# A conditioned decoder layer step on one core: masks and first weights loaded in prompt attention, window keys loaded by position class

## What is computed

```
h = RMSNorm(x) * (1 + scale1) + shift1          scale, shift, gate = silu(c) @ w_ada, split in 6
qa,ka,va,qb,kb,vb,logf,ga,gb = split(h @ w_in)  qa, ka rotated; ga, gb through a sigmoid
A: 3 groups x 4 heads, window and dilation (128,1), (512,4), (2048,16); combined by denominators
   sample rows: query t reads kv[lw + t - d*j], j = 0..window/d, from cache_a1, cache_a2, cache_a3
B: 8 heads, causal, bias = sum of logf between key and query
   sample rows: 16 pages of 128 keys per sequence, picked by page_table from cache_b_k, cache_b_v
mix = (ga * (oA @ w_pa) + gb * (oB @ w_pb)) @ w_o
x   = x + gate1 * RMSNorm(mix);  then a hierarchical mixture of 32 experts, 2 per row
```

## Time and profile before

| what | value |
|---|---|
| median of 3 runs | 1197.81 us (1197.62 to 1199.43) |
| profiled execution, its own time | 1199.27 us |
| its span | 1197.5 us |
| PE busy | 1000.1 us, 84% of the span |
| DVE, ACT, POOL busy | 379.9, 206.0, 187.3 us |
| mean granted clock of PE | 0.91 of full speed |
| read from HBM, written | 335.46 MB, 63.36 MB |

### The profile page before, as it was taken

One profiled execution on the slowest core, in us unless ns is written; L12 is line 12 of the kernel. 1 busy time (PEld: TensorE's weight loads), 2 busy tenths in 40 slices (PEclk: granted clock), 3 DMA queues, 4 the chain that ended last, 5 costly groups with the idle time before them and its releaser, 6 DMA issues. The chain is left out here.

```text
span 1197.5 us, 17987 instructions
## 1 busy us (share of the span) xinstructions
PE 1000.1 (84%) x7324; PEld 585.3 (49%) x7324; DVE 379.9 (32%) x865; ACT 206.0 (17%) x509; POOL 187.3 (16%) x210
## 2 busy tenths in 40 slices
PE   3999999997897169979989997579977998777770
PEld 2444444444564046647656674136554554444430
DVE  3100033237751164516701771003451222100105
ACT  3000000014542011100020003001231211111114
POOL 0000033311200100022222311100003322212110
PEclk9999999999997589989989998669978999989995
DMA  9976666977787779998969984979187999999966
GB/s 339 355 278 248 249 248 248 326 244 255 256 212 168 207 240 213 289 349 322 370 231 334 364 320 151 391 266 341 57 325 269 364 370 383 379 393 394 397 256 237
DMA packets 98062, 348.48 MB, mean 291 GB/s; under 512 B 13018, under 2 KB 56802, under 8 KB 78654
## 3 DMA queue, kind: packets, MB, share of 16 engines
q1 hardware_dynamic: 80478, 265.90, 64.8%
q0 software_dynamic: 15552, 79.97, 18.1%
q10 hardware_dynamic: 1952, 1.48, 0.5%
HBM read 335.46 MB, written 63.36 MB: 333 GB/s over the span
## 5 line engine op out<-in xcount | busy, mean ns | idle before, releaser
L1605 PE MATMUL bank<-turned,w_all 128*128 128x320 f32 (+1 forms) x512 | 143.7, 425 | 0.0
L442 PE MATMUL bank<-w_all,turned 128*128 128x481 f32 (+2 forms) x384 | 119.3, 503 | 1.1 <-DVE turned L651 1.1
L442 PE MATMUL bank<-w_ring,turned 128*128 128x481 f32 (+2 forms) x384 | 118.4, 502 | 0.0
L2013 PE MATMUL bank<-w_all,mix_row 128*64 128x256 f32 x736 | 92.2, 407 | 26.9 <-DMA w_all<-in_w_exp 25.8
L1605 PEld LDWEIGHTS bank<-turned,w_all 128*128 128x128 f32 x512 | 95.3, 196 | 35.6 <-issue 15.5
L2013 PEld LDWEIGHTS bank<-w_all,mix_row 128*64 128x64 f32 x736 | 60.9, 147 | 65.3 <-issue 46.4
L1709 DVE STREAM_TRANSPOSE mods<-w_all 128x2048 f32<-128x2048 f32 (+1 forms) x39 | 86.6, 2239 | 9.8 <-PE bank L1481 7.1
L442 PEld LDWEIGHTS bank<-w_all,turned 128*128 128x128 f32 (+1 forms) x384 | 56.8, 171 | 61.5 <-issue 58.3
L442 PEld LDWEIGHTS bank<-w_ring,turned 128*128 128x128 f32 (+1 forms) x384 | 57.1, 171 | 60.4 <-issue 57.3
L2059 DVE COPY act_t<-bank 128x128 f32<-128x128 f32 x33 | 9.6, 292 | 200.8 <-PE bank L2023 199.1
L661 DVE COPY w_all<-bank 128x481 f32 (+5 forms) x32 | 16.9, 531 | 152.6 <-PE bank L442 152.4
(11 more groups left out here) (357 smaller groups left out, 1318.5 us busy)
## 6 DMA issues: line engine op xcount, KB each, us to landing
w_all<-in_w_exp SPq DMA_DIRECT2D x22, 2048.0 KB, 41.0
out_a_sample<-in_cache_a SPq DMA_DIRECT2D x8, 4080.0 KB, 21.4
w_all<-in_w_exp SPq DMA_DIRECT2D x25, 1024.0 KB, 39.2
mods<-in_w_ada SPq DMA_DIRECT2D x21, 1024.0 KB, 8.8
w_all<-in_cache_a SPq DMA_DIRECT2D x96, 128.0 KB, 7.5
w_all<-in_cache_a SPq DMA_DIRECT2D x40, 256.0 KB, 6.1
turned<-in_w_exp SPq DMA_DIRECT2D x5, 2048.0 KB, 42.2
mods<-in_w_exp SPq DMA_DIRECT2D x5, 2048.0 KB, 43.7
```

The costliest lines, as they stand in the source:

```text
L442: mm = nc.tensor.matmul(m.banks[i][r:r + ROWS[i], 0:hi - lo], m.hT[:, k, i * P:i * P + ROWS[i]], ring[u][:, CW * k + lo:CW * k + hi], star ...
L1605: mm = nc.tensor.matmul(GATE[:, 0:WIDTH[h]], gate_w[b][k][:, c % 2 * P:(c % 2 + 1) * P], m.hT[:, k, 256 * h:256 * h + WIDTH[h]], start=k = ...
L2013: mm = nc.tensor.matmul(m.banks[2 + p][x * SLOTS:(x + 1) * SLOTS, 0:HID], hgT[:, k, :], m.weights(u)[:, (2 * k + x) * HID:(2 * k + x + 1) ...
```

## The change

1. `window_keys_in` takes one residue and one position class of all four sequences per DMA: destination 128 partitions of 256 columns, source [4 sequences, 32 positions, 256]. The number of DMAs stays at 8 per window (4 for the half one), as do their 128 KB.
2. Masks, the gate weights of pair 0 and its merge weights are issued by SP in phase_b, between and behind the early key windows, after a wait for the last turn of the prompt's tiles. The mask input holds the four copies, so it is one DMA. The weights lie in slices of 6 per row tile and not of 7.
3. DVE computes the page row numbers in the first value step, and waits for masks and constants only where a mask is added.
4. The gate pieces start at step 1.

```diff
@@ -113,6 +113,7 @@
+        m.wmask = m.low[4][:, 0:13 * P]
...
@@ -127,6 +128,8 @@
+        m.gate_in = [ctx.enter_context(nc.semaphore(f"gate_w{b}")) for b in range(2)]
+        m.merge_in, m.mask_in = [ctx.enter_context(nc.semaphore(n)) for n in ("merge_w", "mask_rows")]
         with ExitStack() as attn:
...
@@ -212,7 +215,7 @@
-            "mask_window": np.concatenate(window, axis=1), "sample_consts": sample_consts,
+            "mask_window": np.tile(np.concatenate(window, axis=1), (4, 1)), "sample_consts": sample_consts,
...
@@ -245,11 +248,26 @@
 def window_keys_in(eng, I, slot, arrived, u, g):
     name, t, t0 = window_of(g)
     n = min(t, 2)
-    for j in range(4):
-        src = I[name][4 * u + j].rearrange("(c i t) n -> i t c n", c=4, t=t)[:, t0:t0 + n, :, 0:AH * HD]
-        dst = slot[32 * j:32 * j + 32, 0:n * 4 * AH * HD].rearrange("p (t c n) -> p t c n", t=n, c=4)
-        for x in range(n):
-            eng.dma_start(dst[:, x], src[:, x]).then_inc(arrived, 16)
+    src = I[name][4 * u:4 * u + 4].rearrange("s (c i t) n -> s i t c n", c=4, t=t)[:, :, t0:t0 + n, :, 0:AH * HD]
+    for x in range(n):
+        for c in range(4):
+            dst = slot[:, (4 * x + c) * AH * HD:(4 * x + c + 1) * AH * HD]
+            eng.dma_start(dst, src[:, :, x, c]).then_inc(arrived, 16)
+
+
+def gate_weights_in(eng, I, m, p, b):
+    src = I["w_gates"][2 * b + p // 2].rearrange("p (k n) -> p k n", k=KD)[:, :, (p % 2) * 256:(p % 2 + 1) * 256]
+    for lo, hi in ((0, 6), (6, 8)) if b == 0 else ((0, 4), (4, 8)):
+        at = (8 * b + lo) % 6
+        dst = m.low[(8 * b + lo) // 6][:, at * 256:(at + hi - lo) * 256]
+        eng.dma_start(dst.rearrange("p (k n) -> p k n", n=256), src[:, lo:hi, :]).then_inc(m.gate_in[b], 16)
+
+
+def merge_weights_in(eng, I, m, p):
+    cols = slice(256 * p, 256 * (p + 1))
+    for name, lo, hi in (("w_pa", 16, 18), ("w_pb", 18, 22)):
+        dst = m.low[lo // 6][:, lo % 6 * 256:(lo % 6 + hi - lo) * 256].rearrange("p (k n) -> p k n", n=256)
+        eng.dma_start(dst, I[name].rearrange("p (k n) -> p k n", n=D)[:, :, cols]).then_inc(m.merge_in, 16)
 
...
@@ -857,6 +875,14 @@
             for k in range(1, KV_RING - 1):
                 early_keys(k)
                 piece(BEFORE + 1 + k)
+                if k == 2:
+                    sp.dma_start(m.wmask, I["mask_window"]).then_inc(m.mask_in, 16)
+                    sp.wait_ge(turn_a, len(turns))
+                    sp.wait_ge(turn_d, len(turns))
+                    gate_weights_in(sp, I, m, 0, 0)
+                if k == 3:
+                    gate_weights_in(sp, I, m, 0, 1)
+            merge_weights_in(sp, I, m, 0)
 
         @block.gpsimd
         def _(pool):
...
@@ -1230,7 +1256,7 @@
             pieces += [("gate", c, h, 0, 0), ("gate", c, h, 0, 4)]
         for c, h in parts:
             pieces += [("gate", c, h, 1, 0), ("gate", c, h, 1, 4), ("out", c, h, 0, 0)]
-    FIRST, END = 3, 80
+    FIRST, END = 1, 80
...
@@ -1262,16 +1288,16 @@
         share = sb("shares", [P, 4])
-        wmask = m.low[4][:, 0:AT * P]
+        wmask = m.wmask
...
         sc_b = m.sc.rearrange("p (h n) -> p h n", h=2)
-        slices = [m.low[i][:, 256 * x:256 * (x + 1)] for i in range(4) for x in range(7)]
+        slices = [m.low[i][:, 256 * x:256 * (x + 1)] for i in range(4) for x in range(6)]
         gate_w = [slices[0:8], slices[8:16]]
         wp_a, wp_b = slices[16:18], slices[18:22]
-        th_a = {x: slices[22 + x] for x in range(4)}
-        th_b = slices[26:28]
+        th_a = {x: m.low[x][:, 1536:1792] for x in range(4)}
+        th_b = slices[22:24]
         flat_wa = m.wa[:].rearrange("p u f q -> p (u f q)")
         mix = [kept[:, 0], kept[:, 1], *(flat_wa[:, 512 * x:512 * (x + 1)] for x in range(3)), *(m.low[4][:, 512 * x:512 * (x + 1)] for x in range(3))]
...
@@ -1294,7 +1320,7 @@
-        gate_in, wp_in = [sem(f"gate_w{b}") for b in range(2)], sem("merge_w")
+        gate_in, wp_in = m.gate_in, m.merge_in
...
@@ -1337,22 +1363,12 @@
                 (window_keys_in if part == "k" else window_values_in)(sp, I, m.ring[slot_of[n]], arrived(n), own(u), g)
 
             def gate_weights(p, b):
...
+                sp.wait_ge(gate_pe, sum_of[(2 * p - 1, 1, b)] + 1)
+                gate_weights_in(sp, I, m, p, b)
 
             def merge_weights(p):
...
+                sp.wait_ge(out_pe, 4 * p)
+                merge_weights_in(sp, I, m, p)
 
             def past_bias(u, x):
                 if (own(u), x) == (0, 0):
...
@@ -1368,12 +1384,7 @@
 
             sp.dma_start(pt_col[:], I["page_table"].rearrange("a n -> n a")).then_inc(pcol_in, 16)
             window(KV_RING - 1)
-            gate_weights(0, 0)
-            for j in range(4):
-                sp.dma_start(wmask[32 * j:32 * j + 32, :], I["mask_window"]).then_inc(con_in, 16)
             sp.dma_start(consts[:], I["sample_consts"]).then_inc(con_in, 16)
-            gate_weights(0, 1)
-            merge_weights(0)
             sp.dma_start(page_ids, I["page_table"].rearrange("a n -> (a n)").partition_broadcast(P)).then_inc(pages_in, 16)
             sp.dma_start(run_id[:], I["run_ids"]).then_inc(pages_in, 16)
             for t in range(N):
...
@@ -1588,7 +1599,7 @@
-                    pe.wait_ge(wp_in, 48 * (c // 2 + 1))
+                    pe.wait_ge(wp_in, 32 * (c // 2 + 1))
                     pe.wait_ge(gated, 2 * i)
...
@@ -1720,6 +1731,9 @@
+                    dve.wait_ge(m.mask_in, 16)
+                    if c == 3:
+                        dve.wait_ge(con_in, 16)
                     cols = slice(512 * c, 512 * c + (512 if c < 3 else P))
                     ins = add(sc_a[:, cols], S(u, c)[:, 0:cols.stop - cols.start], wmask[:, cols], peak[:, 0, c:c + 1])
                     if c == 3:
...
@@ -1824,14 +1838,15 @@
+            def rows_of_pages():
+                dve.wait_ge(pages_in, 16 * 2)
+                for j in range(4):
+                    rows = slice(32 * j, 32 * j + 32)
+                    for dst, ids in ((key_rows, page_ids[rows].rearrange("p (u s g) -> p u s g", u=2, s=4)[:, :, j, :]),
+                                     (value_rows, page_ids[rows].rearrange("p (s x g) -> p s x g", s=NSEQ, x=4)[:, :, :, j])):
+                        V.tensor_scalar(dst[rows].rearrange("p (a b) -> p a b", a=ids.shape[1]), ids, 32.0, run_id[rows, 0:1], ALU.mult, ALU.add).then_inc(idx_ok, 1)
+
             turn(0)
-            dve.wait_ge(pages_in, 16 * 2)
-            for j in range(4):
...
-            dve.wait_ge(con_in, 16 * 5)
             for t in range(N + 1):
                 for x in piece_at.get(t, []):
                     if x[0] == "out":
...
@@ -1846,6 +1861,8 @@
                         if kind(u) == "b":
                             add_bias(u, 4)
                         maxima(u)
+                    if (u, part, g) == (0, "v", 0):
+                        rows_of_pages()
                     if (u, part, g) == (0, "v", 1):
                         running_sums()
                     if part == "v" and g == 3:
```

More of the change, by code:

```diff
@@ L1339, in gate_weights @@
             def gate_weights(p, b):
[L1340 to L1345, removed]
-            def merge_weights(p):
[L1348 to L1355, removed]
+                sp.wait_ge(gate_pe, sum_of[(2 * p - 1, 1, b)] + 1)
+                gate_weights_in(sp, I, m, p, b)
+            def merge_weights(p):
+                sp.wait_ge(out_pe, 4 * p)
+                merge_weights_in(sp, I, m, p)
             def past_bias(u, x):
@@ L1826, in _ @@
             use_dve = {"shares": shares, "fold": out_cols, "totals": past_sums}
-            turn(0)
-            dve.wait_ge(pages_in, 16 * 2)
-            for j in range(4):
-                rows = slice(32 * j, 32 * j + 32)
-                for dst, ids in ((key_rows, page_ids[rows].rearrange("p (u s g) -> p u s g", u=2, s=4)[:, :, j, :]),
-                                 (value_rows, page_ids[rows].rearrange("p (s x g) -> p s x g", s=NSEQ, x=4)[:, :, :, j])):
-                    V.tensor_scalar(dst[rows].rearrange("p (a b) -> p a b", a=ids.shape[1]), ids, 32.0, run_id[rows, 0:1], ALU.mult, ALU.add).then_inc(idx_ok, 1)
-            dve.wait_ge(con_in, 16 * 5)
+            def rows_of_pages():
[5 more added lines that the diff above has]
+                        V.tensor_scalar(dst[rows].rearrange("p (a b) -> p a b", a=ids.shape[1]), ids, 32.0, run_id[rows, 0:1], ALU.mult, ALU.add).then_inc(idx_ok, 1)
+            turn(0)
             for t in range(N + 1):
```

## The result

The changed kernel takes **1256.38 us** (median of 4 runs, 1253.85 to 1258.95) against 1198.62 us before (4 runs, 1197.62 to 1203.24): a ratio of 1.0474, 95% interval 1.0435 to 1.0513. It is slower, as forecast, and by nearly the forecast amount (1259 us). The profiled execution took 1258.95 us, its span 1257.1.

The account below looks back on a forecast made before the run. The prediction took PE, busy 84% of the span, to bound the kernel, with its longest idle stretch outside the expert part 27.70 us. It summed 1199.3 + 61, less 1.5 for the median, to 1259 us, range 1225 to 1340.

Parts of the forecast that it names:

- Four engines: Key loads: each new key DMA runs on 4 DMA engines, the same four each time, 32 pieces each.
- The price of a window: Key loads: a key window on four engines takes 13 us, between 11.8 and 19.6, against 4.9 before.
- for four engines that walk like rows in step: Key loads: a little added to the 11.8 us window in taking 13 us.
- Step 1: Prompt attention: slice 15 of `w_ada` there at 418, next phase begins at 427 and not 395.0, +32 us.
- The moved loads: Prompt attention: masks and gate weights, 2.95 MB ahead of the last slices of `w_ada`, take 8.4 us.
- Step 2: First unit of cached windows: key window 5 lands at 443, score sum 6 at 453 against 444.31, +9 us.
- the rows of `run_ids` leave the path: First unit: DVE's 25.65 us wait for `run_ids` goes; taken alone, score sum 6 falls 26 us earlier.
- Step 3: Second unit: 6.5 key windows take 84.5 us, last score sum at 561 against 499.57, +61 us.
- Step 4: Behind the second unit: PE is the bound again, nothing is tied to absolute time, so the +61 us stays.
- A: Key loads: rival, all 16 engines at the rate of values, 3 us a window, 1172 us; chance 0.11.
- B: Key loads: rival, four engines hindering each other, 19.6 us a window, 1338 us; chance 0.22.
- C: Whole kernel: rival, window price near 8 us, won wait and slower keys cancel; chance 0.02.

Follow-up runs that it names:

- experiment 3: The kernel before with the new form of the key DMAs and nothing else: 1277.2 us, ratio 1.0673.
- experiment 7: The changed kernel with masks, gate and merge weights issued behind the last slice of `w_ada`: 1243.24 us, ratio 1.0371.
- experiment 1: The changed kernel with the old key loads, one sequence into 32 partitions per DMA: 1183.06 us, ratio 0.9883.
- 4: The kernel before with later page row numbers and the later wait for masks and constants on DVE alone: 1185.94 us, ratio 0.9893.
- experiment 5: The changed kernel with old key loads, and masks, gate and merge weights issued behind the last slice of `w_ada`: 1168.97 us, ratio 0.9772.
- experiment 2: The changed kernel with each key DMA reading 128 rows of one sequence into 128 partitions, keys wrongly placed: 1169.33 us, ratio 0.9783.

## Why the prediction was right

**Four engines.** Right, and now shown by 4 against 2 against 128 in the first place of the source: 94, 48 and 295 GB/s, with 4, 4 and 16 tiny packets to 128 pieces (a DMA of two sequences has 64 pieces and so 2). The Trainium skill's rule in "DMA: Bandwidth & Descriptors", section "Why a DMA increments its semaphore by 16 and not by 1", gives 4, 2 and 16 engines for these, and the trace agrees. Which four they are, no run shows. That they are always the same four follows from the rate, if several key DMAs are in flight together, since on different engines they would have added up to more than 94 GB/s. They are: the window whose last DMA SP has issued by 520.62 is turned at 527.90, after a wait for it, and 7.3 us are five DMAs at 94 GB/s. Nor does the queue run its DMAs one after another: behind the slice issued at 391.65 the DMA share goes from 0.27 (392 to 393 us) to 0.87 (394 to 395), while the slice itself, behind key DMAs on the four engines, is complete only at 402.21.

**The price of a window.** I took 13 us from bounds of 11.8 and 19.6. It measured 11.4, just under the fast bound: an engine of the four moves 94/4 = 23.5 GB/s, where I had 22.1 from value loads. The addition "for four engines that walk like rows in step" was wrong.

**Step 1, prompt attention.** Slice 15 forecast at 418, measured 420.47; first score sum 37.0 us late, forecast 32. Of the 37.0, 3.7 were there at slice 9, so the change made 33.3. The moved loads, 8.4 us in my sum, cost 7.7 against experiment 3 and 6.5 against experiment 7; beside the old keys 9.5 and 9.0 (experiment 1 against 4 and 5), all from slice 9 to 15. Four windows at 11.4 and not 13 should have made it 6 us earlier than forecast. That is not seen. In experiment 3 SP's queue takes 15.0 and 16.2 us for a window with a slice (window issues at 354.15, 369.11 and 385.27), where 11.4 + 3 would be 14.4 and my sum had 16. And the first of the four came later, at 348.97 and not 343.28 (2 us more than the 3.7), behind a window that was slow already and that I had left out.

**Step 2, unit 0.** Sum 6 forecast at 453, measured 460.95: 5 us because the phase began at 432 and not 427, and 4 more because window 5 (issued from 432.58) was turned only at 451.89; the half window behind it took 0.5 us less than I had. In that stretch POOL's own loads for the paged part run as well: from 432 to 441 us they moved 0.73 MB and SP's queue 0.44 MB (one `bias<-in_page_consts` DMA alone took 8.9 us to land). I had counted SP's only. That they are what held window 5 is likely; no run takes them away. That the rows of `run_ids` leave the path was right, and the gain forecast for it with fast keys, sum 6 at 26 us earlier, measured 23.6 in experiment 5.

**Step 3, unit 1.** The last sum forecast at 561, measured 560.93. That is closer than its parts: from sum 6 to the last sum I had 108 us, it was 100.0 (6.5 windows at 11.4 and not 13 are 10 less), and the 8 us late at sum 6 made up for it. Mis-sized terms of both signs cancelled.

**Step 4, the delay stays.** Right: from the last sum of unit 1 to the end of the span the profiled executions of all nine kernels took 689.4 to 697.9 us, the changed kernel 696.2.

So the +61 us of the last sum are +37.0 in prompt attention, -20.4 in unit 0 (46.9 us from first sum to sum 6 before, 26.6 now) and +44.7 in unit 1 (55.3 before, 100.0 now). Less the 3.7 us of slice 9 they are 57.7, which is also what the medians say (1256.38 - 1198.62 = 57.8): the change costs 58 us and not 61.

**The rivals.** A priced the kernel with keys over 16 engines and 128 partitions at 1172 us; experiment 2 is that kernel and took 1169.33. Its arithmetic was good, its premise false: the source's first dimension decides. Its ground in the Trainium skill, "SBUF — State Buffer", section "Door 1: The DMA port swizzle", is about the destination and says nothing of how many engines a DMA gets. Experiment 2 agrees with it (295 against 208 GB/s, though not isolated). A also had the moved loads hidden at 3 us a window; in experiment 2 slice 15 runs at 383.96 after 2.08 us of waiting, so nearly. B, four engines that hinder each other, falls with 23.5 GB/s for each. C had no case.

## What to carry to other kernels

Look at the first dimension of both sides of a DMA before its width: a source that begins with 4 ran on four of 16 engines although the destination was 128 partitions wide, and the count of tiny packets in a trace shows how many engines a form of DMA gets. Loads moved into an earlier phase belong behind the last transfer that this phase still waits for, in the stretch in which the queue would stand empty: the same 3.74 MB cost 7 to 9 us ahead of it in the timelines (12 to 14 by the medians) and nothing that could be seen behind it. Change a load's form alone and read its rate before joining it with a change of order; here the change of order was worth 1.2% (2.3% with the loads behind the last slice) and the form lost 6%.

## What I had not expected of the hardware

Four engines were not slower each than sixteen: 23.5 GB/s on four and 24 on two, against 22.1 in value loads over all 16, in the same pieces of 1 KB, 18.4 in experiment 2 (295/16, where SP's own pace may be the bound), and 13.4 in the old key loads. The share that the profile gives, 0.27 for four engines and 0.136 for two, is close to 4/16 and 2/16, and 1.09 for value loads over all 16 is as much too high, so it can be read as a rough count of engines at work. A slow queue also reaches back to its issuer: the eight DMAs of an early window held SP for 3.65 to 9.57 us before and for 6.97 to 13.95 now. And where the keys are slow, PE's granted clock is low. In the stretch of unit 1's sums, 476 to 500 us, the kernel before has PE busy 21.8 of 24 us at a clock of 1.00 (and experiment 1, with the old keys, 21.6 of 23 us at 1.00); in its own stretch of them, 495 to 561 us, the changed kernel has it busy 33.5 of 66 us, with a wait ahead of each sum, at 0.69. At 0.50, which is the 1.2 GHz level, a score sum takes 1.94 us, and most sums of unit 1 do (in experiment 7 and here) where they took 1.07 before. Not every such stretch is the keys' doing: from 368 to 372 us the clock is 0.50 in the changed kernel, behind a wait of 4.14 us for a slice at 366.36, and it is 0.50 in the kernel before as well, behind 4.12 us at 367.81. PE's busy time in all grew by 19.7 us with the same work.
